# Shifting the high and low halves of the moving rows against each other, stage by stage

## What is computed

```python
for l in range(DEPTH):                                   # DEPTH = 2
    h = h + 0.5 * rmsnorm(swiglu(rmsnorm(h, g[0]), w_in1, w_out1), g[1])
    hn = rmsnorm(h, g[2])
    u_pool, q, k, v, gate_pool, gate_attn = split(hn @ w_in[l])
    y_pool = pool_mixer(u_pool, w_grp, scale, w_pool_proj)
    y_attn = attention(q, k, v, sinks) @ w_attn_proj      # window of 128
    merged = sigmoid(gate_pool) * y_pool + sigmoid(gate_attn) * y_attn
    h = h + rmsnorm(merged @ w_o[l], g[3])
    h = h + 0.5 * rmsnorm(swiglu(rmsnorm(h, g[4]), w_in2, w_out2), g[5])
return h[:, 16:]
```

## Time and profile before

| | |
|---|---|
| median of 3 runs | 1174.79 us (1174.61 to 1175.29) |
| the profiled execution's own time | 1174.66 us |
| its span, first to last instruction | 1172.8 us |
| TensorE busy | 1163.3 us, 99% of the span, 9,269 matmuls |
| VectorE, ScalarE, GpSimd busy | 733.0, 554.8, 430.8 us |
| mean granted TensorE clock | 0.999 |
| HBM traffic | 168 GB/s over the span |

### The profile page before, as it was taken

The page is one execution under the profiler, slowest core; times in us unless marked ns, Lnnn a source line. Parts: engine busy times, 40 slices in busy tenths (PEclk is TensorE's granted clock), DMA queues, the critical chain, the costliest instruction groups (busy, mean ns, idle before and its releaser), DMA issues.

```text
span 1172.8 us, 23880 instructions
## 1 busy us (share of the span) xinstructions
PE 1163.3 (99%) x9269; PEld 1136.1 (97%) x9269; DVE 733.0 (62%) x1145; ACT 554.8 (47%) x818; POOL 430.8 (37%) x486
## 2 busy tenths in 40 slices
PE   9999999999999999999999999999999999999997
PEld 8999999999999999999999999999999999999986
DVE  7655546968666965544586555459676769755542
ACT  7433335637554653333454333356375556533441
POOL 1945500007211286551109555000082122955500
PEclk9999999999999999999999999999999999999999
DMA  9754458372365365535646543573723744654550
GB/s 295 257 179 156 147 179 233 123 232 72 91 190 170 108 216 179 170 121 196 205 134 216 179 157 133 189 226 109 247 82 93 213 145 144 216 179 161 189 170 36
DMA packets 197934, 197.58 MB, mean 168 GB/s; under 512 B 4448, under 2 KB 191200, under 8 KB 197856
## 3 DMA queue, kind: packets, MB, share of 16 engines
q1 hardware_dynamic: 197712, 196.44, 52.4%
q10 hardware_dynamic: 144, 0.05, 0.0%
HBM read 195.43 MB, written 1.05 MB: 168 GB/s over the span
## 4 chain that ended last, share of the span: by engine, by line
PE 92%; issue 3%; DVE 2%; ACT 1%; POOL 0%; DMA 0%; SPq 0%; DVEq 0%; ACTq 0%; POOLq 0%
PE bank L553 27%; PE bank L554 27%; PE bank L555 27%; PE bank L811 2%; PE bank L809 2%; PE bank L810 2%; DVE w_lo L1326 1%; PE bank L898 1%; PE bank L893 1%; PE bank L852 1%; PE bank L588 1%; PE bank L587 1%; PE bank L863 1%; PE bank L615 0%; PE bank L855 0%
## 5 line engine op out<-in xcount | busy, mean ns | idle before, releaser
L553 PE MATMUL bank<-x_hi,w_hi 128*128 128x272 f32 (+1 forms) x1991 | 573.8, 288 | 0.8 <-DVE w_lo L1732 0.8
L554 PE MATMUL bank<-x_lo,w_hi 128*128 128x272 f32 (+1 forms) x1991 | 568.4, 285 | 0.0
L555 PE MATMUL bank<-x_hi,w_lo 128*128 128x272 f32 (+1 forms) x1991 | 568.3, 285 | 0.0
L1009 ACT ACTIVATE w_hi<-raw 128x2048 fp32r<-128x2048 f32 (+3 forms) x201 | 339.0, 1693 | 401.7 <-PE bank L555 388.9
L1326 DVE TENSOR_TENSOR w_lo<-raw,w_hi 128x2048 fp32r<-128x2048 f32 (+3 forms) x203 | 420.3, 2076 | 143.2 <-ACT w_hi L1009 142.9
L553 PEld LDWEIGHTS bank<-x_hi,w_hi 128*128 128x128 f32 x1991 | 377.1, 189 | 1.9 <-issue 0.7
L554 PEld LDWEIGHTS bank<-x_lo,w_hi 128*128 128x128 f32 x1991 | 377.2, 189 | 0.3
L555 PEld LDWEIGHTS bank<-x_hi,w_lo 128*128 128x128 f32 x1991 | 377.1, 189 | 0.0
L1943 POOL TENSOR_TENSOR hid_hi<-silu,up_r 128x272 f32 x88 | 142.5, 1619 | 149.8 <-DVE up_r L1520 144.3
L555 PE MATMUL bank<-hid_hi,w_lo 128*128 128x272 f32 x528 | 151.3, 287 | 0.0
L553 PE MATMUL bank<-hid_hi,w_hi 128*128 128x272 f32 x528 | 151.3, 286 | 0.0
(11 more groups left out here) (219 smaller groups left out, 1323.5 us busy)
## 6 DMA issues: line engine op xcount, KB each, us to landing
raw<-in_ffn_w_in SPq DMA_DIRECT2D x84, 1024.0 KB, 5.0
raw<-in_w_in SPq DMA_DIRECT2D x24, 1024.0 KB, 5.6
raw<-in_ffn_w_out SPq DMA_DIRECT2D x24, 768.0 KB, 4.2
raw<-in_ffn_w_out SPq DMA_DIRECT2D x24, 640.0 KB, 3.9
raw<-in_ffn_w_out SPq DMA_DIRECT2D x10, 1024.0 KB, 5.0
raw<-in_w_in SPq DMA_DIRECT2D x16, 512.0 KB, 5.2
raw<-in_w_attn_proj SPq DMA_DIRECT2D x32, 256.0 KB, 4.3
raw<-in_w_o SPq DMA_DIRECT2D x8, 1024.0 KB, 5.6
```

Of the source, the lines that this page charges most:

```text
L553: pe.matmul(ps[:, t0:T], w[0], a_hi[:, t0:T], start=start, stop=False)
L554: pe.matmul(ps[:, t0:T], w[0], a_lo[:, t0:T], start=False, stop=False)
L555: return pe.matmul(ps[:, t0:T], w[1], a_hi[:, t0:T], start=False, stop=stop)
L1009: last = act.activation(hi, w, ACT.Copy)
```

## The change

Buffers x and hid keep their place and size. What was one fixed slice of a row, floats 0 to 271, becomes a slice that begins at a shift of its own for each layer, stage and half. The tables count in floats of 4 bytes; with the start at 64, the starts modulo 256 become (high/low):

| | layer 0 | layer 1 |
|---|---|---|
| stage 0, first feed-forward in | 64/128 | 72/72 |
| first feed-forward out (hid) | 64/192 | 64/72 |
| stage 1, in-projection | 64/96 | 224/240, from column 16 on 32/48 |
| stage 2, output projection | 80/80 | 32/48 (from column 16 on) |
| stage 3, second feed-forward in | 128/64 | 32/64 (from column 16 on) |
| second feed-forward out (hid) | 192/64 | 64/64, stationary |

The early products keep their rows at shift 0. Other operands, among them o, z and all weights, stay where they are. The remaining hunks put the same call of `x_of` or `hid_of` at the head of each function that reads or writes these rows (`first_three`, `fourth_unit`, `end_out`, `after_kv`, `x_high`, `merge_hi`, `first_operand`, `boundary`, `merge_lo` and GpSimd's `ffn`).

```diff
@@ -69,6 +69,8 @@
 LINE, START = 256, 64
 ROW = -(-T * 4 // LINE) * LINE // 4
+X_SHIFT = (((0, 16), (0, 8), (4, 4), (16, 0)), ((2, 2), (40, 44), (40, 44), (40, 48)))
+HID_SHIFT = (((0, 32), (32, 0)), ((0, 2), (0, 0)))
@@ -187,8 +189,8 @@
-        x_hi = sb("x_hi", [P, KD, ROW], F32R)[:, :, 0:T]
-        x_lo = sb("x_lo", [P, KD, ROW], F32R)[:, :, 0:T]
+        x_hi_rows = sb("x_hi", [P, KD, ROW], F32R)
+        x_lo_rows = sb("x_lo", [P, KD, ROW], F32R)
@@ -264,7 +266,7 @@
-        hid_hi, hid_lo = (ffn_placed[name][0][:, :, 0:T] for name in ("hid_hi", "hid_lo"))
+        hid_hi_rows, hid_lo_rows = (ffn_placed[name][0] for name in ("hid_hi", "hid_lo"))
@@ -407,9 +409,17 @@
         def early_operand(n, which, at):
 
-            hi, lo = (o_hi, o_lo) if n == 1 else (x_hi, x_lo)
+            hi, lo = (o_hi, o_lo) if n == 1 else (x_hi_rows[:, :, 0:T], x_lo_rows[:, :, 0:T])
             slot = (EARLY_OLD, EARLY_OUT)[which] + at
             return hi[:, slot, :], lo[:, slot, :]
+
+        def x_of(l, stage):
+
+            return [rows[:, :, at:at + T] for rows, at in zip((x_hi_rows, x_lo_rows), X_SHIFT[l][stage])]
+
+        def hid_of(l, f):
+
+            return [rows[:, :, at:at + T] for rows, at in zip((hid_hi_rows, hid_lo_rows), HID_SHIFT[l][f])]
@@ -577,6 +587,7 @@
             def deep_three(u, l, q, x_at, starts, banks):
 
+                x_hi, x_lo = x_of(l, {0: 0, 2: 1, 4: 3}[q])
@@ -734,6 +748,8 @@
             def ffn(f, l, t0=0):
+                x_hi, x_lo = x_of(l, 3 * f)
+                hid_hi, hid_lo = hid_of(l, f)
@@ -964,6 +981,7 @@
                     unit(U_AP + m, l, T_AP + 2 * m, (b, b + 1), 4, KD, o_hi, o_lo, t0=t0)
+                x_hi, x_lo = x_of(l, 2)
                 deep_pair(U_WO, l, x_hi, x_lo, lambda k: x_tile(2 * KD + k, l), t=T_WO, t0=t0)
@@ -1411,6 +1432,7 @@
             def x_low(at, columns, k):
 
+                x_hi, x_lo = x_of(*divmod(at // KD, 4))
                 dve.wait_ge(xhi_ready, at + k + 1)
...
```

More of the change, by code:

```diff
@@ L621, in first_three @@
             def first_three():
+                x_hi, x_lo = x_of(0, 0)
                 def product(c, k, low_weights, operand, start=False, stop=False):
@@ L790, in end_out @@
             def end_out(l):
+                hid_hi, hid_lo = hid_of(l, 1)
                 u0 = U_FFN_OUT[1]
@@ L911, in after_kv @@
             def after_kv(l, t0):
+                x_hi, x_lo = x_of(l, 1)
                 for n in range(1, 4):
@@ L1032, in take_root, with x_high @@
                 act.activation(root[:, 0:3], post_var[:, 0:3], ACT.Sqrt).then_inc(root_done, 1)
-            def x_high(columns, h_before, k):
+            def x_high(n, columns, h_before, k):
+                x_hi, _ = x_of(n // NORMS, {0: 0, 2: 1, 4: 3}[n % NORMS])
                 act.wait_ge(h_ready, h_before + k + 1)
@@ L1056, in pre_norm @@
                         act.wait_ge(early_done, n // 2)
-                    x_high(columns, h_before, k)
+                    x_high(n, columns, h_before, k)
                     if k == EARLY_OUT:
@@ L1196, in merge_hi @@
             def merge_hi(m, l):
+                x_hi, _ = x_of(l, 2)
                 act.wait_ge(merged, l * KD + m + 1)
@@ L1203, in first_operand @@
             def first_operand(k):
+                x_hi, _ = x_of(0, 0)
                 act.activation(x_hi[:, k, :], h[:, k, :], ACT.Copy, scale=g_all[:, k:k + 1]).then_inc(xhi_ready, 1)
@@ L1443, in boundary @@
                 spread = small[:, S_BC:S_BC + T]
+                x_hi, _ = x_of(*divmod(at // KD, 4))
                 def normed(k, first=0, end=T):
```

## The result

The changed kernel takes 1184.38 us (median of 4 runs, 1184.31 to 1185.2) against 1174.81 us before: a ratio of 1.0083, 95% interval 1.0071 to 1.0095. It is 9.6 us slower. The profiled execution is the longest of the four, 1185.20 us, so the profiles show some 1.0 us more of a loss than the medians do. The prediction was 1170.2 us with a range of 1160 to 1177, and 0.17 on a slower kernel.

A forecast was written before the change was run, and what follows sets the result against it. The prediction took TensorE's matmuls times their start-to-start step as the bound. From the profiled 1174.66 us it took 3.3 (part 1) and 1.2 (part 2), with 0 for parts 3 and 4: 1170.2 us, range 1160 to 1177.

The forecast's parts named there:

- What bounds the kernel: TensorE, whole kernel: time is almost wholly the number of matmuls times the step; TensorE busy 1163.3 of 1172.8 us.
- Part 1: Layer 1's 256-column stages, 1,770 matmuls: halves leaving 128/128 for unequal starts save 1.85 ns each, 3.3 us less.
- Part 2: 4,128 matmuls of 272 columns, halves now apart: 0.3 ns less each, 1.2 us less; ends -9.5 and +8.3 us.
- Part 3: Layer 0's output projection, layer 1's first feed-forward and its hid, both halves moved (nearly) alike: 0; ends -4.1, +5.9 us.
- Part 4: ScalarE, VectorE and GpSimd writing the x and hid halves at the new addresses: 0 change.
- A: Rival, slower: at 272 columns halves apart cost what o and z show, 2.0 ns more; 1179.7 us, chance 0.17.
- B: Rival, no difference: constant distance between repeating rows is worth nothing, savings come from walking rows alone; 1174.7 us, chance 0.12.
- C: Rival, larger gain: neighbours at different offsets save at 272 columns what z saves at 256; 1161.1 us, chance 0.15.

The follow-up runs named there:

- the map: Table of steps from follow-up runs with both halves at one start, by the row's start less the weights' start modulo 256; 123.3 to 126.7 ns at 272 columns.

## Why the prediction was wrong

**What bounds the kernel: right.** Time is matmuls times step. 10.2 of 10.6 us were found in the steps.

**Part 1, 256 columns, -3.3 us: right in size, and partly by luck.** Measured -0.9, -0.2 and -2.2, together -3.3 us; stage 3 at 117.8 ns where I had expected 118.2. But I had put the gain down to halves that lie apart. Equal halves gain too (118.7 ns at 0/0, 113.3 with both 64 ahead): what gained was leaving the weights' own place, where both halves had lain.

**Part 2, 272 columns with halves apart, -1.2 us: wrong, and the step that failed.** Measured +1.1 + 0.8 + 5.6 + 0.6 + 0.6 + 0.2 = +8.9 us, just past the upper end of +8.3. I had written that the 2.0 ns of o and z "goes with rows that walk, which the new rows do not". The runs show that at 272 columns a row loses at every place tried outside the band of 64 to 96 bytes ahead of the weights, walking or not: equal, resting rows at 192 read 126.7 ns, more than the walking ones. The walking rows look like an average over good and bad places: the map's prices for the eight starts of `o_hi` average 125.4 to 125.8 ns, an estimate, where o took 125.3. That made them the better guide, and I set them aside on a difference that no row had shown to matter. That the sum came so near the upper end is luck again: 2.0 ns everywhere was not what happened, but 5.6 ns in one stage and some 1.1 ns in most others.

**Part 3, both halves moved alike, 0: wrong.** Measured +0.6 + 3.4 + 0.6 = +4.6 us, inside its bound of +5.9. I took the nearest place, 64, for the nearest price. Eight bytes further, at 72, the step is already 126.7 ns. A price with an edge in it is not met by the nearest row, and that bound belonged in the range's sum with part 2's: +8.3 + 5.9 - 3.3 would have reached 1185.6 us.

**Part 4, the writers: right.** 496 and 519 ns at the new addresses for 495 and 519, GpSimd's three 3.5 us a tile for 3.6; TensorE's waits grew by 0.6 us.

**The rivals.** A had the right sign and 1179.7 us. Its mechanism, halves apart, was half of the truth: the largest loss after layer 0's stage 3 came from halves that lie together. B is out: layer 1's shifts alone gave 0.22%, interval 0.9967 to 0.9988, and rows that rest gained there. C's mechanism, a saving at 272 columns, is out: no run went under 123.3 ns at that length. At 256 columns there was more to be had than C said: 6.7 ns a matmul at 64 ahead, with both halves there and the quick step, where the change put only the low half there. By the rule of the Trainium skill named in the prediction, a fixed 2.5 ns a matmul, there could be neither loss nor gain; the smallest surcharge that any long stretch here shows is 113.3 - 106.7 = 6.7 ns.

The same page of the Trainium skill ("TensorE: Matmul & The Clock Gate", section "Step-by-step: what each phase is for") says that the moving operand and the weights have read ports of their own, so that loading the next weights takes nothing from the running matmul. What the runs show is hard to fit with that, though they do not show the cause: with the rows at one address and the weights moved by 64 bytes, the 272-column step went from 123.3 to 126.7 ns and the 256-column step from 120.0 to 113.3.

**Open.** Why 64 ahead is cheap, what the edge between 64 and 56 ahead is, why one place has two steps and what picks one of them, and why the mixed pair 128/64 is dearer than either of its rows in some stretches (128.9 ns) and not in others (124.4 to 124.6). That the weights' load and the moving row's reads meet in the memory would fit it, and is argued, not shown: no run took the weight loads away.

## What to carry to other kernels

Where TensorE is the bound and each matmul loads new weights, measure the step from start to start in an unbroken stretch, and try the moving operand's start against the weights' start modulo 256 bytes, for each number of columns by itself, and in more than one execution, since one place can have two steps; a column offset in the access counts as part of the start. An untouched operand at other offsets is a price list that is already in the trace: don't explain it away without a row. Before you bound a step by its nearest neighbour, ask whether the price could have an edge there.

## What the hardware showed that I had not expected

The step between matmuls of the same size ranges from 113.3 to 120.0 ns at 256 columns and from 123.3 to 128.9 at 272, at a clock of 1.00 throughout. In most long stretches three steps add up to a multiple of 8 cycles of 2.4 GHz: 888, 896, 912 and 928 cycles at 272 columns, 816, 848 and 864 at 256. It is no rule: 114.43/913 = 125.3 ns makes 902 cycles and 109.05/919 = 118.7 ns makes 854.

One place can have two steps. At 256 columns they are 113.3 and 117.8 ns, 64 ahead of the weights and 64 past them; at 272 columns and level with the weights 125.2 and 126.7. In layer 1's stage 3 a stretch of 923 matmuls keeps one of the two from its first to its last matmul, which is worth 4.1 us; in stage 1 they change from tile to tile within one execution. Single executions of one program differ by 4 to 6 us, and the two steps are the likely reason for most of it.
